# A two-layer hybrid decoder step: padded expert slots move no rows, results are scattered by token and loaded back as blocks

## The reference, cut to what matters

```python
def moe(x, router_w, router_bias, w_gate, w_up, w_down):
    xt = x.reshape(-1, D)                                  # D = 1024
    scores = sigmoid(xt @ router_w)                        # 16 experts in 4 groups
    sel = (scores + router_bias).reshape(-1, 4, 4)
    g = argmax(top_k(sel, 2)[0].sum(-1))                   # the best group
    idx = top_k(masked_to_group(sel, g), 2)[1]             # its 2 best experts
    gate = take(scores, idx); gate = gate / gate.sum(-1)
    w = (one_hot(idx, 16) * gate[..., None]).sum(1)
    hg = einsum('nd,edf->nef', xt, w_gate)                 # f = 256
    hu = einsum('nd,edf->nef', xt, w_up)
    hh = silu(hg) * hu * w[:, :, None]
    return einsum('nef,efd->nd', hh, w_down)

x = layer_norm(ALPHA * x + moe(x, ...), ln2_g[l], ln2_b[l])
```

## Time and profile before

| what | us |
|---|---|
| median of 3 runs | 1742.96 |
| lowest, highest | 1740.89, 1758.02 |
| the profiled execution, its own time | 1750.55 |
| its span | 1748.8 |

### The profile page before, as it was taken

The page is one execution under the profiler, slowest core; times in us unless marked ns, Lnnn a source line. Parts: engine busy times, 40 slices in busy tenths (PEclk is TensorE's granted clock), DMA queues, the critical chain, the costliest instruction groups (busy, mean ns, idle before and its releaser), DMA issues.

```text
span 1748.8 us, 19440 instructions
## 1 busy us (share of the span) xinstructions
PE 1435.4 (82%) x7575; PEld 939.8 (54%) x7575; DVE 696.9 (40%) x1381; ACT 433.9 (25%) x945; POOL 123.8 (7%) x157
## 2 busy tenths in 40 slices
PE   2999997799899579999099999869889966999950
PEld 2767765466667444444077676546666753444420
DVE  3542463556422532222544246345652153223217
ACT  2221211355302312222133111035441140212110
POOL 1000001200100010000210000120010001000002
PEclk9989985899999779999599899579999986999985
DMA  8320102101360149997532010130134104999935
GB/s 273 72 49 25 37 25 55 63 10 61 121 191 2 52 133 346 324 349 233 172 67 61 25 37 25 30 88 10 61 121 149 69 4 161 321 302 350 300 109 165
DMA packets 190988, 220.73 MB, mean 126 GB/s; under 512 B 47992, under 2 KB 164168, under 8 KB 188712
## 3 DMA queue, kind: packets, MB, share of 16 engines
q1 hardware_dynamic: 173800, 152.25, 28.8%
q0 software_dynamic: 12336, 49.82, 8.1%
q10 hardware_dynamic: 4752, 17.30, 2.5%
HBM read 187.48 MB, written 31.83 MB: 125 GB/s over the span
## 4 chain that ended last, share of the span: by engine, by line
PE 64%; DMA 13%; DVE 9%; issue 6%; ACT 3%; SPq 2%; DVEq 1%; POOL 1%; ACTq 1%; POOLq 0%; PEldq 0%
PE ps L510 14%; DMA over<-in_moe_w_up 9%; PE ps L1014 8%; PE ps L943 7%; PE ps L465 6%; PE ps L1030 3%; SPq L2193 2%; PE ps L713 2%; PE ps L780 2%; PE ps L643 2%; DMA y_rows<-over 1%; PE ps L898 1%; PE ps L822 1%; DVE zT L2058 1%; PE ps L640 1%
## 5 line engine op out<-in xcount | busy, mean ns | idle before, releaser
L1095 ACT ACTIVATE over<-ps 128x512 f32<-128x512 f32 (+11 forms) x390 | 186.4, 508 | 520.2 <-PE ps L510 157.7
L1014 PE MATMUL ps<-over 128*128 128x512 f32 x512 | 235.5, 614 | 26.6 <-DMA over<-in_moe_w_up 24.8
L510 PE MATMUL ps<-xT,wslot 128*128 128x296 f32 x960 | 256.6, 427 | 0.0
L510 PEld LDWEIGHTS ps<-xT,wslot 128*128 128x128 f32 x960 | 186.6, 197 | 58.7 <-issue 7.0
L465 PE MATMUL ps<-const,over 128*128 128x128 f32 (+4 forms) x992 | 152.1, 287 | 74.0 <-DVEq L418 20.1
L465 PEld LDWEIGHTS ps<-const,over 128*128 128x128 f32 (+4 forms) x992 | 117.6, 143 | 124.5 <-issue 46.7
L1014 PEld LDWEIGHTS ps<-over 128*128 128x128 f32 x512 | 97.8, 196 | 143.9 <-issue 115.0
L2018 DVE TENSOR_SCALAR over<-over 128x256 f32<-128x256 f32 x33 | 9.7, 294 | 292.3 <-ACT over L1384 267.5
L1441 DVE COPY over<-ps 128x512 f32<-128x512 f32 (+5 forms) x134 | 68.7, 521 | 124.7 <-PE ps L510 67.6
L1030 PE MATMUL ps<-over 128*128 128x512 f32 x256 | 115.3, 593 | 1.2 <-DVE over L1441 1.2
L1384 ACT ACTIVATE over<-ps 128x256 f32<-128x256 f32 x32 | 12.3, 384 | 253.4 <-PE ps L1014 253.4
(11 more groups left out here) (381 smaller groups left out, 1919.9 us busy)
## 6 DMA issues: line engine op xcount, KB each, us to landing
over<-in_moe_w_gate SPq DMA_DIRECT2D x33, 1024.0 KB, 9.8
over<-in_moe_w_up SPq DMA_DIRECT2D x33, 1024.0 KB, 12.2
over<-in_moe_w_down SPq DMA_DIRECT2D x33, 1024.0 KB, 6.4
y_rows<-over ACTq DMA_DIRECT2D x33, 512.0 KB, 7.3
wslot<-in_w_in SPq DMA_DIRECT2D x30, 512.0 KB, 4.0
y_rows<-over SPq DMA_DIRECT2D x1, 4608.0 KB, 13.5
wslot<-in_w_out SPq DMA_DIRECT2D x8, 512.0 KB, 3.7
over<-in_w_out SPq DMA_DIRECT2D x8, 512.0 KB, 6.6
```

The source lines that it names most:

```text
L510: i = mm(b[:, 0:HALF], wslot[:, u % NSLOT, k, :], xT[:, k, SH[h]], start=(k == 0), stop=(k == KD - 1))
L1014: i = mm(b, xgT[:, e % 2, k, :], wgu[:, e % 2, k, :], start=(k == 0), stop=(k == KD - 1))
L1095: rel(f_(dst, src, ACT.Copy), key, "A")
```

## The change

Padded slots get an index outside the buffer, and gathers and scatters carry a bound past which an index is skipped. For each slot a second number is made, 2·token + (0 or 1), the row of `y_rows` that the result goes to; `y_rows` shrinks from 3,200 rows to 1,184. GpSimd scatters the results by these numbers (`put_y`), in place of ScalarE's store: the scatter of e-4 stands behind the gather of e in its queue, the last four behind the gather for the overflow. The combine reads blocks of 128 tokens with both rows of each (8 KB per partition), five loads from SP's queue, ahead of the next layer's weight loads. The clearing of `y_rows`, its memset and SP's wait go.

```diff
+NO_SLOT = 8192
-    put("token", np.where(token < T, token, 0))
+    put("ids", np.stack([np.where(token < T, v - NO_SLOT, 0) for v in (token, 2 * token, token, 2 * token + 1)], 1)
+        .reshape(P, 2, 2, TT).transpose(0, 1, 3, 2))
...
-        y_rows = nc.dram_tensor("y_rows", [NTILE * P, D], F32, kind="Internal").ap()
+        y_rows = nc.dram_tensor("y_rows", [2 * T, D], F32, kind="Internal").ap()
...
-                    i = mm(b[:, 0:NTILE], row_hot[:, n, :], tile_hot[:, n, :], start=(n == 0), stop=(n == 2 * TT - 1))
+                    i = mm(b[:, 0:2 * NTILE], row_hot[:, n, :], tile_val[:, n, :, :], start=(n == 0), stop=(n == 2 * TT - 1))
...
                     act.drain().then_inc(S("y_copied"), 1)
-                    act.wait_ge(S("y_copied"), n + 1)
-                    act.dma_start(y_rows[e * P:(e + 1) * P, :], yt[:, e % 2, :]).then_inc(S(f"y_written{e % 2}"), 16)
...
-                        act.wait_ge(S(f"over_y_{l}"), k + 1)
-                        act.dma_start(y_rows[(E + k) * P:(E + k + 1) * P, :], yt[:, 0, :]).then_inc(S(f"over_written_{l}"), 16)
...
-                for x in range(2):
-                    th = tile_hot[:, x * TT:(x + 1) * TT, :]
-                    tt(th, th, cst("token").unsqueeze(2).to_broadcast([P, TT, NTILE]), ALU.mult)
+                tt(tile_val, tile_hot.unsqueeze(2).to_broadcast([P, 2 * TT, 2, NTILE]),
+                   cst("ids").rearrange("p (n v) -> p n v", v=2).unsqueeze(3).to_broadcast([P, 2 * TT, 2, NTILE]), ALU.mult)
                 sig("slot_onehots")
-                v.tensor_copy(slot, slotf)
-                sig("slots_ready")
...
-                copy(("ids", l), fetch, bank(("ids", l))[:, 0:NTILE])
+                rel(ts_(fetch, bank(key)[:, 0:2 * NTILE].rearrange("p (v n) -> p v n", v=2), float(NO_SLOT), None, ALU.add), key, "D")
...
-                        dve.wait_ge(S(f"y_fetched{n}"), 16 * (l + 1))
+                        dve.wait_ge(S(f"y_fetched{t}"), 16 * (l + 1))
...
-            g.memset(over[:, 0:D], 0.0)
...
+                def fetch_x(dst, e):
+                    return g.indirect_dma_start(dst, None, x_rows, rows_at(fetch[:, 0, e:e + 1]), bounds_check=T - 1, oob_is_err=False)
+
+                def put_y(src, e):
+                    return g.indirect_dma_start(y_rows, rows_at(fetch[:, 1, e:e + 1]), src, None, bounds_check=2 * T - 1, oob_is_err=False)
+
+                def put_expert(e):
+                    pool.wait_ge(S("y_copied"), l * E + e + 1)
+                    put_y(yt[:, e % 2, :], e).then_inc(S(f"y_written{e % 2}"), 16)
+
                 for e in range(E):
                     if e >= 3:
                         pool.wait_ge(filled, index[("xg", l, e - 3, 1)] + 1)
-                    g.indirect_dma_start(xg[:, e % 3, :], None, x_rows, rows_at(fetch[:, e:e + 1])).then_inc(S(f"x_fetched{e % 3}"), 16)
+                    fetch_x(xg[:, e % 3, :], e).then_inc(S(f"x_fetched{e % 3}"), 16)
+                    if e >= 4:
+                        put_expert(e - 4)
...
                     fetch_overflow(0)
+                for e in range(E - 4, E):
+                    put_expert(e)
                 barrier(pool, "pool")
...
+                        pool.wait_ge(S(f"over_y_{l}"), k + 1)
+                        put_y(yt[:, 0, :], E + k).then_inc(S(f"over_written_{l}"), 16)
...
-                pool.wait_ge(S("slots_ready"), l + 1)
-                for t in range(TT):
-                    q = rows_of(t)
-                    for x in range(2):
-                        n = 2 * t + x
-                        g.indirect_dma_start(yg[0:q, n, :], None, y_rows, rows_at(slot[0:q, x, t:t + 1])).then_inc(S(f"y_fetched{n}"), 16)
...
-            ld(y_rows[E * P:NTILE * P, :].rearrange("(i p) d -> p i d", p=P), over[:, 0:D].unsqueeze(1).to_broadcast([P, NOVER, D]), "rows_cleared")
...
-            sp.wait_ge(S("rows_cleared"), 16)
...
                 overflow(0, count)
                 barrier(sp, "sp")
+                for t in range(TT):
+                    q = rows_of(t)
+                    ld(yg[0:q, 2 * t:2 * t + 2, :], y_rows[2 * t * P:2 * (t * P + q), :].rearrange("(p a) d -> p a d", a=2), f"y_fetched{t}")
```

More of the change, by code:

```diff
@@ L347, in build @@
         tile_hot = moe.get(2 * TT, NTILE)
+        tile_val = moe.get(2 * TT, 2, NTILE)
         row_hot = moe.get(2 * TT, P)
-        slot = sb("slot", [P, 2, TT], I32)
         logT = moe.get(2 * P)
-        fetch = sb("fetch", [P, NTILE], I32)
+        fetch = sb("fetch", [P, 2, NTILE], I32)
         dyn = sb("dyn", [P, NOVER + 1], I32)
@@ L2006, in _ @@
                 sig("overflow_known")
-                copy(("ids", l), fetch, bank(("ids", l))[:, 0:NTILE])
+                key = ("ids", l)
+                full(dve, key)
+                rel(ts_(fetch, bank(key)[:, 0:2 * NTILE].rearrange("p (v n) -> p v n", v=2), float(NO_SLOT), None, ALU.add), key, "D")
                 sig("ids_ready")
@@ L2157, in _ @@
                         pool.wait_ge(filled, index[("xg", l, e - 3, 1)] + 1)
-                    g.indirect_dma_start(xg[:, e % 3, :], None, x_rows, rows_at(fetch[:, e:e + 1])).then_inc(S(f"x_fetched{e % 3}"), 16)
+                    fetch_x(xg[:, e % 3, :], e).then_inc(S(f"x_fetched{e % 3}"), 16)
+                    if e >= 4:
+                        put_expert(e - 4)
                 def fetch_overflow(k):
-                    g.indirect_dma_start(xg[:, 1, :], None, x_rows, rows_at(fetch[:, E + k:E + k + 1])).then_inc(S(f"over_fetched_{l}"), 16)
+                    fetch_x(xg[:, 1, :], E + k).then_inc(S(f"over_fetched_{l}"), 16)
                 pool.wait_ge(S("overflow_known"), l + 1)
```

## The result

The changed kernel takes 1768.65 us, median of 20 runs (1759.24 to 1774.55); the kernel before takes 1746.33, median of 20 (1734.46 to 1760.44). The ratio is 1.0124, 95% interval 1.0104 to 1.0144: slower by more than 1%, where 1730 us, faster or the same, had been forecast. The profiled execution has a span of 1762.7 us (before 1748.8). The two traces are only 13.9 us apart where the medians are 22.3 apart, because the profiled execution of before took 4 us more than its median (1750.55) and that of after 4 us less (1764.48).

The account below looks back on a forecast made before the run. TensorE, busy 82%, was taken as the bound, so savings counted only where it stands still (24.8 us of weight waits in the stages). -8.0 + 0 - 4 + 2.9 - 3.6 = -12.7 off 1742.96 gave 1730 us, range 1711 to 1740.

Parts of the forecast that it names:

- The start: Before layer 0: without the clearing the barrier opens 6.5 us earlier, and a fuller clock saves 1.5: -8.0 us.
- Routing: Both layers' routing: small changes in product, slot matmul, list and first gather cancel out: 0 us.
- The expert stage: Both layers' experts: skipped rows lighten the DMA load, but little if the first rows' engines stay full: -4 us.
- last stores: Ends of the expert stages and overflow: scatters land later than ScalarE's stores, +1.2, +1.2 and +0.5: +2.9 us.
- the rival as written: GpSimd's indirect issues grow long because the bound is compared for each index: +21.6 us, 1765 us, chance 0.09.
- The quarter of the even case: Expert stage: share of the even saving kept because memory and port see fewer bytes: the -4 us.
- the even case: Expert stage: skipped rows spread evenly over 16 DMA engines, each of 16 waits 1.14 us shorter: -18.2 us.
- signs named for the changed profile: Barrier near 33, clock near 1.00, fewer indirect packets, up weights near 12 us, waits some 20, one combine wait.
- Combine: Combine in both layers: one load brings both rows, so VectorE starts earlier and skips the second wait: -3.6 us.
- Even relief: Rival: the expert stage gives 18.2 us, total -26.9, so 1716 us; chance 0.32.
- No rows saved: Rival: skipped rows still cost packets or reads, expert stage 0, total -8.7, so 1734 us; chance 0.13.

Follow-up runs that it names:

- e4: Changed kernel with the clearing transfer, its memset and SP's wait put back, into a buffer nobody reads: 1777.98 us, ratio 1.0197.
- e13: Kernel before with the bound on all its gathers of hidden rows, no index outside it and every row moved: 1801.26 us, ratio 1.0298.
- e18: Kernel before with the bound on the gathers of experts 3 to 15 alone: 1793.85 us, ratio 1.0284.
- e10: Changed kernel with two products of constants on TensorE before the wait of each odd expert from 3 on: 1748.36 us, ratio 1.0023.
- e14: Kernel before with SP issuing gate and up weights of e+1 ahead of the down weights of e: 1714.83 us, ratio 0.9808.
- e2: Changed kernel with filled slots spread evenly over the tile's 128 positions by reversed bits: 1738.74 us, ratio 0.995.
- e1: Changed kernel with the scatter of e-5, not e-4, behind the gather of e, so gathers leave earlier: 1761.72 us, ratio 1.009.
- e8: e1 with another mapping, an expert's first 64 ranks at positions 0 to 31 and 64 to 95: 1727.03 us, ratio 0.9851.
- e7: e1 with nothing skipped: padded slots gather row 591 and scatter to rows of their own, bound kept: 1790.09 us, ratio 1.0232.
- e5: Kernel before with only its gathers of hidden rows skipping padded slots, by a bound: 1775.92 us, ratio 1.0136.
- e3: Changed kernel with the edits of e1 and e2 together: 1729.75 us, ratio 0.9917.
- e11: e5 with the filled slots spread over the tile as in e2, the combine's slot numbers moved along: 1757.74 us, ratio 1.0067.
- e6: Kernel before with each expert's plain store issued by GpSimd behind its gathers, not by ScalarE: 1754.09 us, ratio 1.003.
- e9: Kernel before with SP issuing gate and up weights only once the result of e-3 is copied: 1746.94 us, ratio 0.9999.

## Why the prediction was wrong

**The start (-8.0) held.** The barrier opened at 33.55 (forecast near 33.0), ScalarE was late next, as said, and the clock behind it was 1.00. Putting the clearing back costs 9.3 us (e4), and the traces with and without it are 8.7 us apart at the first gather.

**Routing (0) held in its parts.** The product of 500 elements took 0.67 us (forecast 0.65), and the 20 slot matmuls, now of 50 columns, took 4.51 (before 4.48). Not seen was the first gather's issue, 1.47 us for 0.94: it lands after 4.74 us and not 4.12, where -0.2 was forecast.

**The expert stage (-4, with 0 to -9 for its own range, -18.2 at the end) failed.** With the last stores (+2.9), which fall in the same stretch, -1.1 was forecast and +29.5 measured, some 31 us off. Three steps of it were wrong.

1. "An issue costs 0.94 us, 1.63 at most, two an expert of 11.5: hidden, as long as both stay under about 5.5." A bound was priced only as a rival that sets in when an issue passes 2.7 us. The issue grew by 0.05 us (e13), and the rival as written is refuted: the longest was 1.49. That its 1765 us lie so near the measured 1768.65 is chance. But the bound, which makes a gather 0.54 us late, cost 52 us (e13) on all gathers and 46 on those of experts 3 to 15 (e18). GpSimd's own time stayed hidden, as said; what the bound does to the arrival of the weights had no term in the sum.
2. The wait was taken as the only thing that a later landing changes. The runs show two more. The clock is lower behind a longer wait: `up` takes 7.13 us behind 1.80 (clock 1.00), 8.83 behind 2.67 (clock 0.81 from 655 to 664) and 9.90 behind 4.83 (0.71 from 729.4 to 739 in e13), and keeping TensorE busy gives 20.3 us back (e10). And a landing that runs on longer shares more with the next batch, as read in one pair of e13. So 24.8 us was not all that the stages can give: e14 gives them 31 in its trace. The sum of TensorE's waits and its `up` blocks, 260.3 us before (24.8 and 235.5), follows the times: 284.6 after (+24; time +22), 310.2 in e13 (+50; +52), 232.1 in e14 (-28; -35).
3. "If an engine's part goes by position in the tile, those with the first rows carry as much as before and the others nothing", so nearly no gain. The place in the tile does count (30 us in e2, 35 from e1 to e8), but the conclusion failed, and which engine moves which row was the author's estimate, which no view shows. The quarter of the even case in the -4, for fewer bytes at memory and port, was an estimate too, and no run takes it by itself. Skipping with the filled slots in front gives 28 us with scatters (e7 to e1) and 25 for the gathers alone (e13 to e5). Spreading them gives 32 more (e1 to e3), or 18 (e5 to e11). So evenly spread skipping is worth about 60 us to a kernel whose gathers carry the bound (e7 to e3; 44 for the gathers alone, e13 to e11), because it takes away what steps 1 and 2 add. Against the kernel before, which has no bound, the stages of e3 are only 9.1 us shorter in the traces, later last stores included, some 13 without them. The even case of -18.2 was not far off, then, and its total of 1716 was not reached (1729.75).

The parts roughly add up: 52 for the bound, -28 for the skipping, +7 for the order in GpSimd's queue (e1), and -9 at the start make +22, the measured difference. Each was taken in another surrounding, and the sum has no place for the 6 us of e6, the last stores or the combine, so the agreement is in part luck.

Of the signs named for the changed profile, the barrier near 33, the clock behind it and the single wait before the combine came. The up weights landed after 13.0 us in the median of the whole run and not near 12, TensorE waited 32.3 us and not some 20, and the packets of the indirect queue, expected to fall, rose, while its bytes fell.

**Last stores (+2.9).** In layer 0 the load of the combine leaves 9.84 us after the last copy's end (833.82 to 843.66), where the gather left 7.96 after (830.97 to 838.93): +1.9, forecast +1.2. In layer 1 TensorE starts on the overflow 10.74 us after that copy and not 8.30: +2.4, forecast +0.5. Behind the overflow's own copy the step is 3.5 us before and after: 0, forecast +1.2. The sum is +4.3 for +2.9. The scatter starts 0.8 us behind the copy, being on another engine and behind a register move. No scatter took more than 1.03 us to issue.

VectorE was idle during the last scatter of each layer and the overflow's (0.97 us each). The first gathers take 1.47 and 1.49 us beside its work, and 0.94 and 0.95 in the same place where they have no bound (e18). Of the 20 issues of the combine of before three were long, 1.63, 1.59 and 1.21 us, against a median of 0.94.

**Combine (-3.6).** In layer 0 VectorE starts 5.33 us after the issue (forecast 5.1; before 5.74), and both adds follow each other without a wait: -1.5, forecast -1.8. In layer 1 it starts after 5.15 us where 4.45 had been enough, and saves a wait of 1.47: -0.8. The sum is -2.3.

**The rivals.** Even relief as worked out (waits under 8 us, landings of 11) is seen in no version with the rows in front and SP's order of loads as it was. No rows saved is refuted, by bytes and by 28 us. The range, 1711 to 1740, missed by 29 us, since no case held a price for what the bound does to the weights' arrival.

**What stays open.** That the bound costs is shown; how 0.54 us at the gather becomes 15.3 in place of 12.5 us at the weights is not. Two readings were at hand: the smaller lead over the weights, or a longer transfer, since bounded indices might be processed more slowly. The second has the rows against it: the bounded gather lands as soon after its start as the other (5.2 and 5.3 us in the median, e13 and before), and the packets of the queue take 8.0% of 1800.9 us and 8.1% of 1748.8, nearly the same time. The first is only argued, and cannot be the whole: the lead is 2.70 us in e11 as well, where most up weights land after 12.2 us. The kernel before with each gather held back by half a microsecond and no bound would tell. It was not run, nor were bounded gathers with later weights; e9 moved the weights by only 0.3 us.

## What to carry to other kernels

Where a stage's transfers take about as long as the compute that they feed, price an edit by what it does to the arrival of the transfer waited for, not by bytes or by an engine's busy time: a bound that makes the instructions of an engine that is 7% busy half a microsecond later cost 3% here. Before adding or saving traffic, look whether the critical load can leave earlier; two weight loads exchanged in SP's order brought 35 us to the kernel before, 60 to the changed one and made nearly all other differences vanish. When rows of a tile are left out, spread the ones that stay over its positions: that gave 30 us here (e2).

## What the runs showed of the hardware that was not expected

- A bound on an indirect transfer brings a register move and makes the instruction start 0.49 us later after a wait and last 0.99 in place of 0.94 us. The first gather of a layer lasts 1.47 us with it; where the first one with a bound is a layer's fourth (e18), it lasts 1.01.
- A skipped row keeps its packet and loses its bytes: 14400 packets for 42.24 MB in the changed kernel and 14400 for 57.43 MB in e7, where nothing is skipped.
- Where the filled rows of an indirect transfer stand in the tile counts. Up weights land after 12.5 us in the median with them in front (e1), after 11.2 with them spread (e3) and after 11.2 with the first 64 at positions 0 to 31 and 64 to 95 (e8, 35 us better than e1).
- TensorE with two products of constants ahead of each long wait is faster by 20 us than without (e10): `up` then takes 7.1 us and not 8.8.
